# Low parts of the weights for four k-tiles at once, and the tiles behind the gates two at a time

## What is computed

```
x = x + moba(rmsnorm(x) ) @ w_o                       # softmax attention, 16 heads of 64
x = x + (silu(conv3(h @ up_a)) * conv3(h @ up_b)) @ down     # h = rmsnorm(x), width 2816
x = rmsnorm(x)
x = x + 0.5 (1 + gate1) * (silu(h @ w_gate) * (h @ w_up)) @ w_down    # h = modulated rmsnorm
x = x + (1 + gate2) * (8 stick-breaking heads and 8 forgetting heads) @ w_o
x = x + 0.5 (1 + gate3) * (silu(h @ w_gate) * (h @ w_up)) @ w_down
```

## Time and profile before

| | |
|---|---|
| median of three runs | 831.11 us |
| the profiled execution: its time, its span | 829.95 us, 827.7 us |
| TensorE busy | 801.8 us, 97% of the span |
| VectorE busy | 644.9 us, 78%, 1331 instructions |
| ScalarE busy | 488.5 us, 59%, 1015 instructions |
| low parts of the weights (L931) | 528 instructions, 343.3 us |
| high parts of the weights (L688) | 528 instructions, 308.3 us |

### The profile page before, as it was taken

One profiled execution on the slowest core, in us unless ns is written; L12 is line 12 of the kernel. 1 busy time (PEld: TensorE's weight loads), 2 busy tenths in 40 slices (PEclk: granted clock), 3 DMA queues, 4 the chain that ended last, 5 costly groups with the idle time before them and its releaser, 6 DMA issues. The chain is left out here.

```text
span 827.7 us, 16827 instructions
## 1 busy us (share of the span) xinstructions
PE 801.8 (97%) x6818; PEld 779.6 (94%) x6818; DVE 644.9 (78%) x1331; ACT 488.5 (59%) x1015; POOL 21.1 (3%) x53
## 2 busy tenths in 40 slices
PE   6999997999999999999999999799999999999998
PEld 5899997999999999999999999789889999999998
DVE  5788877889899887999888887868657897765651
ACT  6755556766767565755555556665656765555440
POOL 1000000000000000000000000600000000000000
PEclk9999999999999999999999999999999999999999
DMA  8776673765565987499998876446343677665540
GB/s 287 257 233 233 200 245 118 242 202 191 196 224 172 325 298 253 152 304 334 348 321 296 295 252 213 131 128 192 106 137 103 204 234 255 224 204 192 191 154 27
DMA packets 150014, 179.44 MB, mean 217 GB/s; under 512 B 5681, under 2 KB 139569, under 8 KB 149937
## 3 DMA queue, kind: packets, MB, share of 16 engines
q1 hardware_dynamic: 148624, 178.17, 65.6%
q0 software_dynamic: 1024, 0.03, 0.1%
q10 hardware_dynamic: 288, 0.16, 0.1%
HBM read 177.27 MB, written 1.05 MB: 215 GB/s over the span
## 5 line engine op out<-in xcount | busy, mean ns | idle before, releaser
L931 DVE TENSOR_TENSOR wlo<-raw,whi 128x512 fp32r<-128x512 f32 x528 | 343.3, 685 | 69.1 <-ACT whi L688 68.4
L1305 PE MATMUL bank<-A,whi 128*128 128x256 f32 x1280 | 363.9, 284 | 12.3 <-DVE wlo L931 7.5
L688 ACT ACTIVATE whi<-raw 128x512 fp32r<-128x512 f32 x528 | 308.3, 622 | 100.2 <-PE bank L1307 94.5
L1306 PE MATMUL bank<-A,whi 128*128 128x256 f32 x1280 | 356.8, 279 | 0.0
L1307 PE MATMUL bank<-A,wlo 128*128 128x256 f32 x1280 | 356.7, 279 | 0.0
L1305 PEld LDWEIGHTS bank<-A,whi 128*128 128x128 f32 x1280 | 243.0, 190 | 15.6 <-DVE wlo L931 9.0
L1306 PEld LDWEIGHTS bank<-A,whi 128*128 128x128 f32 x1280 | 243.0, 190 | 1.0 <-issue 1.0
L1307 PEld LDWEIGHTS bank<-A,wlo 128*128 128x128 f32 x1280 | 243.0, 190 | 0.0
L1305 PE MATMUL bank<-Hhi,whi 128*128 128x256 f32 x528 | 146.0, 276 | 0.0
L1306 PE MATMUL bank<-Hlo,whi 128*128 128x256 f32 x528 | 145.7, 276 | 0.0
L1307 PE MATMUL bank<-Hhi,wlo 128*128 128x256 f32 x528 | 145.7, 276 | 0.0
(11 more groups left out here) (148 smaller groups left out, 784.2 us busy)
## 6 DMA issues: line engine op xcount, KB each, us to landing
...
```

The lines of the kernel that those rows point to most:

```text
L688: act.activation(whi[:, i % SPL, k0:k1, 0:width], raw[:, i % RAW, k0:k1, 0:width], ACT.Copy).then_inc(s_whi, 1)
L931: dve.tensor_tensor(lo, raw[:, i % RAW, k0:k1, 0:width], hi.bitcast(F32), ALU.subtract).then_inc(s_wlo, 1)
L1305: pe.matmul(o, hi, xh, start=kg == 0 and not (j and halved(g)), stop=False)
L1306: pe.matmul(o, hi, xl, start=False, stop=False)
```

## The change

- The low parts of the weights in the up and down phases are made for four k-tiles by one instruction (128 x 1024 in place of two of 128 x 512). `low_part` names the pair whose "lo" step carries both; the step of the even pair is dropped, and the matmuls of all four k-tiles wait for the one that stays, at the place of the odd pair. A slab of six k-tiles ends with a single pair. High parts stay as they are.
- `Hhi` and `Hlo` become one 128 x 512 instruction each for a group. In up1 the Silu and `hb` do too. In up2 and up4 `hb` and Silu read PSUM and stay two instructions, but count the semaphore once, after the second; s_h0 is gone.
- In qkv1 an eviction is one 128 x 512 instruction, with the norm's factor broadcast over the two tiles.

```diff
--- before.py
+++ after.py
@@ -94,6 +94,11 @@
 QKV3_TILE = {0: 0, 512: 8, 1024: 16, 1536: 4, 2048: 12, 2560: 20}
 
 
+def low_part(slabs, i, q):
+
+    return min(q | 1, slabs[i][4] // 2 - 1) if slabs[i][0][:2] in ("up", "do") else q
+
+
 def qkv_base(ph, c0):
     return c0 // P if ph == "qkv1" else QKV3_TILE[c0 // 512 * 512] + (c0 % 512) // P
 
@@ -142,7 +147,8 @@
 
         def lower():
             i, q, final = rounded.pop(0)
-            st.put("lo", i, q)
+            if q == low_part(slabs, i, q):
+                st.put("lo", i, q)
             if final:
                 st.put("load", i + RAW)
 
...
@@ -544,7 +550,7 @@
         def emptied(need, g):
 
             if g in by_silu:
-                need.wait_ge(s_silu, 2 * silu_g[g])
+                need.wait_ge(s_silu, silu_g[g])
             elif g >= 0:
                 need.wait_ge(s_evicted, nth_evicted[g])
 
@@ -810,8 +816,7 @@
                     elif part == 3 and tag == "cg":
                         emptied(need, g)
                         silu()
-                        for i in range(2):
-                            act.activation(ca[:, i, :], ca[:, i, :], ACT.Silu).then_inc(s_silu, 1)
+                        act.activation(ca[:, 0:2, :], ca[:, 0:2, :], ACT.Silu).then_inc(s_silu, 1)
                     elif part == 3:
                         hidden_hi(g)
                 elif tag == "g" and g not in unnormed:
@@ -819,12 +824,14 @@
                     emptied(need, g - 1)
                     silu()
                     for i in range(2):
-                        act.activation(ca[:, i, :], at(g, i), ACT.Silu).then_inc(s_silu, 1)
+                        ins = act.activation(ca[:, i, :], at(g, i), ACT.Silu)
+                    ins.then_inc(s_silu, 1)
                 elif tag == "g":
                     emptied(need, g)
                     silu()
                     for i in range(2):
-                        act.activation(ca[:, i, :], ca[:, i, :], ACT.Silu, bias=bcol[:, i:i + 1]).then_inc(s_silu, 1)
+                        ins = act.activation(ca[:, i, :], ca[:, i, :], ACT.Silu, bias=bcol[:, i:i + 1])
+                    ins.then_inc(s_silu, 1)
                 elif tag == "u" and part == 1:
                     hidden_hi(g)
 
@@ -838,13 +845,11 @@
             def hidden_hi(g):
                 ph, tag, c0 = groups[g]
                 n = 2 * (c0 // C)
-                need.wait_ge(s_h0, pair_g[g])
-                act.activation(Hhi[:, n, :], hb[:, 0, :], ACT.Copy).then_inc(s_hhi, 1)
                 if tag == "cu":
                     need.wait_ge(s_h1, pair_g[g])
                 else:
                     emptied(need, g)
-                act.activation(Hhi[:, n + 1, :], hb[:, 1, :], ACT.Copy).then_inc(s_hhi, 1)
+                act.activation(Hhi[:, n:n + 2, :], hb[:, :, :], ACT.Copy).then_inc(s_hhi, 1)
 
             def first_passes(n):
                 first_pass(n)
@@ -926,6 +931,8 @@
 
             def weights(i, q):
                 width, k0, k1 = slabs[i][6], 2 * q, 2 * q + 2
+                if q % 2 and low_part(slabs, i, q - 1) == q:
+                    k0 -= 2
                 hi, lo = whi[:, i % SPL, k0:k1, 0:width], wlo[:, i % SPL, k0:k1, 0:width]
                 need.wait_ge(s_whi, nth("hi", i, q))
                 dve.tensor_tensor(lo, raw[:, i % RAW, k0:k1, 0:width], hi.bitcast(F32), ALU.subtract).then_inc(s_wlo, 1)
@@ -1043,10 +1050,10 @@
                 if tag == "qkv" and ph == "qkv1":
                     have_r(ph)
                     scl = 0.125 if c0 < D else 1.0
-                    for i in range(2):
-                        ins = dve.scalar_tensor_tensor(out=QKV[:, c0 // P + i, :], in0=at(g, i), scalar=scl,
-                                                       in1=Rr[:, 0, :], op0=ALU.mult, op1=ALU.mult)
-                    ins.then_inc(s_evicted, 1)
+                    both = banks[2 * (g % 2)][:, :].rearrange("p (a c) -> p a c", a=2)
+                    r = Rr[:, 0, :].unsqueeze(1).broadcast_to([P, 2, S])
+                    dve.scalar_tensor_tensor(out=QKV[:, c0 // P:c0 // P + 2, :], in0=both, scalar=scl, in1=r,
+                                             op0=ALU.mult, op1=ALU.mult).then_inc(s_evicted, 1)
                 elif tag == "qkv" and g not in unnormed:
                     base = qkv_base(ph, c0)
                     scl = 0.125 if c0 < 512 else 1.0
@@ -1085,14 +1092,9 @@
                             ins.then_inc(s_evicted, 1)
                     elif part == 3 and tag == "cu":
                         emptied(need, g)
-                        need.wait_ge(s_hlo, 2 * pair_g[g] - 2)
-                        for i in range(2):
-                            need.wait_ge(s_silu, 2 * silu_g[g - 1] - 1 + i)
-                            ins = dve.tensor_tensor(hb[:, i, :], ca[:, 2 + i, :], ca[:, i, :], ALU.mult)
-                            if i == 0:
-                                ins.then_inc(s_h0, 1)
-                            else:
-                                ins.then_inc(s_h1, 1)
+                        need.wait_ge(s_hlo, pair_g[g] - 1)
+                        need.wait_ge(s_silu, silu_g[g - 1])
+                        dve.tensor_tensor(hb[:, :, :], ca[:, 2:4, :], ca[:, 0:2, :], ALU.mult).then_inc(s_h1, 1)
                     elif part == 4:
                         hidden_lo(g)
                 elif g in by_silu:
@@ -1101,20 +1103,17 @@
                     have_r(ph)
                     for i in range(2):
                         dve.tensor_tensor(ca[:, i, :], at(g, i), Rr[:, 0, :], ALU.mult).then_inc(s_scaled, 1)
-                    need.wait_ge(s_silu, 2 * silu_g[g] - 2)
+                    need.wait_ge(s_silu, silu_g[g] - 1)
                     for i in range(2):
                         ins = dve.tensor_copy(bcol[:, i:i + 1], at(g, i, S, S + 1))
                     ins.then_inc(s_evicted, 1)
                 elif tag == "u" and g not in unnormed:
                     if part == 0:
-                        need.wait_ge(s_hlo, 2 * pair_g[g] - 2)
+                        need.wait_ge(s_hlo, pair_g[g] - 1)
+                        need.wait_ge(s_silu, silu_g[g - 1])
                         for i in range(2):
-                            need.wait_ge(s_silu, 2 * silu_g[g - 1] - 1 + i)
                             ins = dve.tensor_tensor(hb[:, i, :], at(g, i), ca[:, i, :], ALU.mult)
-                            if i == 0:
-                                ins.then_inc(s_h0, 1)
-                            else:
-                                ins.then_inc(s_evicted, 1)
+                        ins.then_inc(s_evicted, 1)
                     elif part == 4:
                         hidden_lo(g)
                 elif tag == "u":
@@ -1170,9 +1166,8 @@
 
             def hidden_lo(g):
                 n = 2 * (groups[g][2] // C)
-                for i in range(2):
-                    need.wait_ge(s_hhi, 2 * pair_g[g] - 1 + i)
-                    dve.tensor_tensor(Hlo[:, n + i, :], hb[:, i, :], Hhi[:, n + i, :].bitcast(F32), ALU.subtract).then_inc(s_hlo, 1)
+                need.wait_ge(s_hhi, pair_g[g])
+                dve.tensor_tensor(Hlo[:, n:n + 2, :], hb[:, :, :], Hhi[:, n:n + 2, :].bitcast(F32), ALU.subtract).then_inc(s_hlo, 1)
 
             def evict_f(g):
                 p = slice(96, 104)
@@ -1269,7 +1264,7 @@
                     need.wait_ge(s_olo, (0 if ph == "o1" else 8) + kg + 1)
                     return Ohi[:, kg, :], Olo[:, kg, :], S
                 if tag == "down":
-                    need.wait_ge(s_hlo, KF * FFN_OF[ph] + kg + 1)
+                    need.wait_ge(s_hlo, KF // 2 * FFN_OF[ph] + kg // 2 + 1)
                     return Hhi[:, kg, :], Hlo[:, kg, :], S
                 if g in unnormed:
                     need.wait_ge(s_alo, 8 * NORM_OF[ph] + kg + 1)
@@ -1288,7 +1283,7 @@
                 final = last and kt == nk - 1
                 if tag == "ot":
                     g, kg, final = g - 2 + kt % 3, k0 + kt // 3, kt > 2
-                need.wait_ge(s_wlo, nth("lo", i, kt // 2))
+                need.wait_ge(s_wlo, nth("lo", i, low_part(slabs, i, kt // 2)))
                 xh, xl, ncol = here(tag, ph, kg, g)
                 if kg == 0 and tag == "o" and c0 >= 2 * C:
                     need.wait_ge(s_exp, soft[(12 if ph == "o1" else 28) + c0 // C - 2])
```

2 lines of the change are left out of this document (1 added, 1 removed).

## The result

The changed kernel takes 836.19 us (median of 12 runs, 834.98 to 841.88); the kernel before, run beside it, 832.59 us (12 runs). The ratio is 1.006, with a 95% interval from 1.0043 to 1.0077: 3.6 to 6.4 us slower, about 5. (The plain difference of the two medians is 3.6 us, the low end of that interval.) The forecast was 2.6 us slower. The profiled execution took 835.49 us, 5.54 more than the one before it.

A forecast was written before the change was run, and what follows sets the result against it. TensorE, busy 801.8 of 827.7 us, was taken as the bound. Terms 1.2 + 0.3 + 0.9 + 0.2 = 2.6 us took the median from 831.11 to 833.7 us; range 832.0 to 835.4, eight in ten 831.0 to 836.0.

The forecast's parts named there:

- Up1, the new stop: Slab 17, 25th matmul: TensorE waits for the merged low part and starts 1.64 us later; up1 costs 1.2 us net.
- Giving back: Up1 at 158.71: the 0.45 us wait for a convolution shrinks as TensorE comes later; 0.4 us taken, at the least nothing.
- Behind the gates: Up1: `Hlo` starts 0.50 us later after `hb`, mostly free; the stop of 0.33 at 236.31 grows about 0.3 us.
- Low parts elsewhere: Down phases and rest of up: low parts ready six to thirteen microseconds ahead, four at the least left; no cost.
- Up2: Beginning of up2: the stop of 0.40 at 344.06 grows by 0.9 us (0.5 to 1.2), all on the path.
- Up4: End of o3 gains 0.7 us at 644.40, later pieces cost 0.9; the stop at 671.02 comes 0.2 us later.
- Nothing in qkv1, the down phases and at the end: Qkv1 evictions 0, at most 0.3 us gained; down phases' low parts early enough; the kernel's end has no low parts.
- the clock: Rival 1, up1: the new 1.64 us stop lowers TensorE's clock once more, 1.6 us extra, 835.3 us; chance 0.12.
- VectorE was not ahead at the late stops: Rival 2 claimed fewer instructions put VectorE ahead at all five late stops, at most 3.04 us, 828.1 us; chance 0.06.
- the third: Rival 3: it cancels, up1 stop against whole o3 gain, 236.31 and up2 unchanged; 831.3 us; 0.14 together with the fourth.
- the fourth: Rival 4: merging does nothing, TensorE's clock and matmuls alone decide; 831.1 us; 0.14 together with the third.

## Why the prediction failed

The terms were 1.2 (up1), 0.3 (behind the gates in up1), 0.9 (up2) and 0.2 (up4), 2.6 us in all; in the traces they are 0.6, 2.8, 1.33 and 0.4, with 0.4 in qkv3 and o3, 5.5 in all. The absolute time missed by 2.5 us (836.19 for 833.7), of which 1.5 are the starting point: three runs had given 831.11 us for the kernel before, twelve give 832.59.

- **Up1, the new stop** (1.64 us): right in place, cause and size, 1.71 measured. Giving back: 0.4 us was the stop of 158.71; measured 1.11 from slab 20 to 23. The stop had been followed by two slabs at the slow pace, in which I saw only the stop; so it did not hold that everywhere else in the up and down phases a matmul starts each 0.113 us.
- **Behind the gates** (0.3 us in up1): this is the step that failed. "Where VectorE has time until the next slab, this costs nothing; in most of up1 it has more than half a microsecond." It had 10.88 - 10.73 = 0.15 us in each round, and the change takes 0.37: the merged gates alone take 0.32, the merged low parts alone 0.24. The 0.50 us behind `hb` itself was right (0.70 us idle, in 32 places). I had looked at a single place for idle time and taken ScalarE's part of the loop for slack; the round, which two rows of one operation give at once, I had not measured. From slab 23 to slab 39 the slip grew by 2.8 us, where I had 0.3: 2.4 of it are waits, the new stop at 216.12, the growth at 239.46 and short ones, and 0.4 are the slow pace of slabs 33 and 34. The growth of the one stop that I had named was about right (0.36 for 0.3). The loss is not the gates' alone: both parts of the change use up the same 0.15 us, and each alone has fewer waits (0.8 and 0.2 us) than both together.
- **Low parts elsewhere** (leaving "four at the least", so nothing): the same error a second time. For TensorE's need of the low parts that held: only in slab 17 did a stop end with one. But low parts also stand in the way of evictions, and there a merged pair that is not ready until its second tile is rounded lets VectorE stand still for 1.22 instead of 0.71 us in each round. By itself this makes a round of 10.97 us and 1.65 us from slab 23 to 39, half of it waits.
- **Up2**: 0.9 us said, 1.33 measured, the stop at 348.42 growing by 0.94 as said, and the one behind it, at 354.93, which I had not looked at, giving the rest.
- **Up4**: -0.7 at the end of o3 and +0.9 later said; -0.91 and +1.31 measured.
- **Nothing in qkv1, the down phases and at the end**: right, within 0.1 us. For qkv3 and o3 nothing was forecast either, and 0.4 us came, with no cause shown.
- **The rivals**: the clock did not fall again behind the stop in slab 17. VectorE was not ahead at the late stops: only that of 158.71 went, as TensorE came later. Of the third, the gain at the end of o3 was whole, but up2 and 236.31 did not stay as they were. Against the fourth, the loss is in waits that end with VectorE; that the pace of TensorE alone moves times by 1 or 2 us, whatever the edit, was in none of them. By the Trainium skill's advice on few operations (VectorE: DVE Perf Modes, "Rules for kernel authors") the change should have gained; VectorE's time did fall, by 19.4 us, and apart from about 0.1 us at the end of o3 no gain on TensorE's path is seen from it.
- The busy time of VectorE, 625.5 us, was forecast at 633. The rows of the low parts fall from 342.0 to 230.8 + 93.8 us, 0.09 us for each of the 192 merges. I had put in 0.05, which was read from low parts that follow each other without a wait.
